# Two halves of weights split ahead of the last turn, and the branch of TensorE with the uncrowded path first

## The reference

```python
p_group = softmax(h @ router_group)            # 4 groups
pg_top, g_idx = top_k(p_group, 1)              # one group for each token
logits_e = (h @ router_expert).reshape(b, s, 4, 4)
sel = logits of the chosen group's 4 experts
top_vals, top_idx = top_k(sel, 2)              # two experts of it
combine = one_hot(expert_id) * pg_top * softmax(top_vals)
for e in range(16):
    hid = silu(h @ w_gate[e]) * (h @ w_up[e])  # 2048 x 512 each
    y = y + combine[:, e] * (hid @ w_down[e])  # 512 x 2048
```

## Time and profile before

| | us |
|---|---|
| median of three runs | 2960.05 (2958.6 to 2963.99) |
| span of the profiled execution | 2960.2 |
| TensorE busy | 2919.3 (99%) |
| TensorE weight loads | 2566.1 (87%) |
| VectorE busy | 1932.5 (65%) |
| ScalarE busy | 1649.3 (56%) |
| stretch from the last attention unit to the first expert unit | 781 to 799.3 |
| experts | 799.3 to 1401 |

### The profile page before, as it was taken

How to read it: one execution, slowest core, us unless ns; L and a number is a source line. 1 busy time by engine, 2 the same in 40 slices (tenths; PEclk the granted TensorE clock), 3 DMA queues, 4 the chain that set the end, 5 groups by cost and what they waited for, 6 DMA issues and landing times.

```text
span 2960.2 us, 40967 instructions
## 1 busy us (share of the span) xinstructions
PE 2919.3 (99%) x16760; PEld 2566.1 (87%) x16760; DVE 1932.5 (65%) x2257; ACT 1649.3 (56%) x1957; POOL 105.6 (4%) x83
## 2 busy tenths in 40 slices
PE   8999999999899999999999999999999999999998
PEld 8988988898777878777999988888899999888886
DVE  6777444535698989898676764555656577555554
ACT  6544444435587877777555544554545654445453
POOL 2222000000000000000000000000000000000000
PEclk9999999999999999999999999999999999999999
DMA  7544566545498989899555556555564555555553
GB/s 267 179 142 161 203 207 237 206 168 174 134 358 311 362 314 357 313 353 317 196 170 187 166 176 197 189 177 184 181 205 143 191 166 185 191 190 190 181 195 128
DMA packets 279930, 632.52 MB, mean 214 GB/s; under 512 B 18953, under 2 KB 32834, under 8 KB 262466
## 3 DMA queue, kind: packets, MB, share of 16 engines
q1 hardware_dynamic: 278274, 624.67, 61.6%
q10 hardware_dynamic: 1184, 4.20, 0.4%
q0 software_dynamic: 288, 1.05, 0.1%
HBM read 622.52 MB, written 7.36 MB: 213 GB/s over the span
## 4 chain that ended last, share of the span: by engine, by line
PE 84%; DVE 6%; issue 5%; ACT 4%; DMA 1%; SPq 0%; POOL 0%; POOLq 0%; ACTq 0%; DVEq 0%
PE pairs L662 17%; PE pairs L664 17%; PE pairs L663 17%; PE pairs L672 8%; PE pairs L676 8%; PE pairs L674 8%; DVE w_lo L1983 3%; PE misc L1143 2%; ACT w_hi L1384 1%; PE misc L821 1%; PE misc L1073 1%; PE misc L1029 1%; ACT scratch L1798 1%; DVE scratch L2664 1%; DMA raw<-in_w_gate_dram 0%
## 5 line engine op out<-in xcount | busy, mean ns | idle before, releaser
L1983 DVE TENSOR_TENSOR w_lo<-raw,w_hi 128x1024 fp32r<-128x1024 f32 x1136 | 1388.1, 1243 | 855.0 <-ACT w_hi L1384 847.0
L1384 ACT ACTIVATE w_hi<-raw 128x1024 fp32r<-128x1024 f32 x1136 | 1183.7, 1059 | 952.6 <-PE pairs L664 585.0
L662 PE MATMUL pairs<-w_hi,a_hi 128*128 128x512 f32 x1664 | 658.5, 396 | 5.4 <-DVE a_lo L2417 2.4
L664 PE MATMUL pairs<-w_hi,a_lo 128*128 128x512 f32 x1664 | 648.4, 390 | 0.0
L663 PE MATMUL pairs<-w_lo,a_hi 128*128 128x512 f32 x1664 | 648.1, 389 | 0.0
L672 PE MATMUL pairs<-a_hi,w_hi 128*128 128x256 f32 x1920 | 551.2, 287 | 6.6 <-DVE w_lo L1983 6.6
L674 PE MATMUL pairs<-a_lo,w_hi 128*128 128x256 f32 x1920 | 544.1, 283 | 0.0
L676 PE MATMUL pairs<-a_hi,w_lo 128*128 128x256 f32 x1920 | 544.0, 283 | 0.0
L662 PEld LDWEIGHTS pairs<-w_hi,a_hi 128*128 128x128 f32 x1664 | 312.5, 188 | 77.7 <-DVE w_lo L1983 11.5
L672 PEld LDWEIGHTS pairs<-a_hi,w_hi 128*128 128x128 f32 x1920 | 369.2, 192 | 11.1 <-DVE w_lo L1983 6.9
L674 PEld LDWEIGHTS pairs<-a_lo,w_hi 128*128 128x128 f32 x1920 | 369.4, 192 | 0.7 <-issue 0.2
(11 more groups left out here) (353 smaller groups left out, 2250.5 us busy)
## 6 DMA issues: line engine op xcount, KB each, us to landing
raw<-in_w_in_dram SPq DMA_DIRECT2D x232, 1024.0 KB, 5.2
raw<-in_w_out_dram SPq DMA_DIRECT2D x80, 1024.0 KB, 5.1
raw<-in_w_gate_dram SPq DMA_DIRECT2D x64, 1024.0 KB, 5.6
raw<-in_w_up_dram SPq DMA_DIRECT2D x64, 1024.0 KB, 5.6
raw<-in_w_down_dram SPq DMA_DIRECT2D x64, 1024.0 KB, 6.1
raw<-in_xattn_wk_dram SPq DMA_DIRECT2D x16, 1024.0 KB, 5.1
raw<-in_xattn_wv_dram SPq DMA_DIRECT2D x16, 1024.0 KB, 5.0
raw<-in_xattn_wq_dram SPq DMA_DIRECT2D x16, 1024.0 KB, 5.1
```

Of the source, the lines that this page charges most:

```text
L662: nc.tensor.matmul(o, hi[:, k, tok], w_hi[:, s, q, :], start=k == 0, stop=False)
L664: m = nc.tensor.matmul(o, lo[:, k, tok], w_hi[:, s, q, :], start=False, stop=last)
L1384: a.activation(w_hi[:, i % HSLOTS], raw[:, i // 2, 2 * (i % 2):2 * (i % 2) + 2, :], ACT.Copy).then_inc(hi_done, 1)
L1983: v.tensor_tensor(w_lo[:, i % HSLOTS], raw[:, i // 2, 2 * (i % 2):2 * (i % 2) + 2, :], w_hi[:, i % HSLOTS].bitcast(F32), ALU.subtract).the ...
```

## The change

ScalarE splits four halves (0 to 3 of the first expert unit) ahead of its wait for the last turn, and none behind `by_row_copy(3)`. VectorE splits three halves ahead of `add_unit("wo", 3)` and the fourth behind it, and none in the two places in the choice. In `slots` the product `slot_of` comes first, then the maximum, then `choose(0)`, and only then the number for the branch. That number is now `roomy`: 1 when the largest count is at most 128. TensorE's branch tests it and has `experts(1)` as its first body and `experts(TT)` as its second.

```diff
-        crowded = SC[:, 12994:12995].bitcast(I32)
+        roomy = SC[:, 12994:12995].bitcast(I32)
...
             pe.wait_ge(crowd_ok, 1)
-            many = nc.values_load(crowded[0:1, 0:1], engines=[pe.engine], min_val=0, max_val=P)
-            with pe.If(many):
+            few = nc.values_load(roomy[0:1, 0:1], engines=[pe.engine], min_val=0, max_val=1)
+            with pe.If(few):
+                experts(1)
+            with pe.Else():
                 experts(TT)
-            with pe.Else():
-                experts(1)
...
-            run(2)
+            run(4)
             act.wait_ge(turned, 16)
...
-            run(2)
             act.wait_ge(rt_x, 1)
             a.activation(rt_ge, rt_gd, ACT.Exp).then_inc(rt_e, 1)
...
             v.tensor_scalar(upto, causal[:], -0.5, None, ALU.is_ge)
-            run(2)
+            run(3)
             add_unit("wo", 3)
+            run(1)
             for k in range(4):
...
                 dve.wait_ge(rank_mm, 1)
-                s1(v.tensor_reduce(fullest, misc[:, 1, 8:12], AX.X, ALU.max))
-                v.tensor_scalar(crowded, fullest, -float(P), 0.0, ALU.add, ALU.max)\
-                 .then_inc(crowd_ok, 1)
                 s1(v.tensor_tensor(slot_of, misc[:, 1, 0:8].rearrange("p (t e) -> p t e", t=TT), rt_og,
                                    ALU.mult))
+                step(v.tensor_reduce(fullest, misc[:, 1, 8:12], AX.X, ALU.max))
                 choose(0)
+                step.wait()
+                v.tensor_scalar(roomy, fullest, float(P), None, ALU.is_le).then_inc(crowd_ok, 1)
...
             group_choice()
             slots()
-            run(1)
             expert_choice()
-            run(1)
             first_lo(0, 0)
```

## The result

The changed kernel takes 2963.89 us (median of 21 runs, 2961.37 to 2973.13), the kernel before 2960.91 us (median of 21, 2958.38 to 2963.99). The ratio is 1.0014, 95% interval 1.0008 to 1.0020: slower by 2.4 to 5.9 us (the two medians lie 3.0 us apart). The forecast was 2960.0 us, no change. The time lies inside the range, but the interval leaves out the forecast: a loss was measured where none was foreseen. The 21 runs of each kernel tell apart less than the 0.2% that the prediction took for the limit.

The account below looks back on a forecast made before the run. TensorE, busy 99%, bounds the kernel; only its wait before the experts, behind the taken branch and VectorE's chain, could be won. 2960.2 − 1.6 + 1.5 = 2960.1, against the median 2960.0 us; range 2957.0 to 2964.5.

Parts of the forecast that it names:

- The branch at the front: TensorE's branch before the experts: not taken, it costs 0.076 us instead of 3.418, hidden by the gathering matmuls.
- VectorE's chain: Before the experts: VectorE's splits of halves 2 and 3 leave the choice; TensorE's first expert matmul comes 1.9 us earlier.
- the first unit: First expert unit: VectorE moves less than TensorE, so `turn_pick` waits 0.3 us and 1.6 us of gain are left.
- The halves split ahead: Around `wo`'s end: ScalarE's and VectorE's early splits fit idle time and cost nothing; without cover, routing starts up to 0.4 us later.
- the transfers: SyncE's transfer for halves 2 and 3 goes at about 783, not 797.6; counted nothing, bounds 2.8 us gain, 1 us loss.
- The jump at the end: End of `experts(1)`, between lru0 0 and lru0 1: a taken jump of 3.42 us, partly hidden by the sequencer's lead.
- The lead is 2.1 us, eighteen matmuls of 0.12 us: Ahead of unit lru0 1: TensorE's sequencer runs 2.1 us ahead of the matmuls, hiding that much of the exit jump.
- 1.5 us lost: Exit jump's net cost: 1.3 us bare beyond the lead plus about 0.2 us for the first issue behind it.
- 0 to 0.1 us: Behind the exit jump, until the next small matmuls: further cost, since little lead is regained but none is needed.
- a second fetch: Named in the chances only: slower by over 0.2%, chance 0.05, needs the clock and the bare jump, or this.
- the rival with a chance of 0.08: At about 1426, TensorE's clock halves for 10.2 us after the bare 1.5 us, losing 4.4 us: 2964.4 us; chance 0.08.
- The upper bound of 3.7 us for a jump with no lead: Exit jump: the most it was said to lose, 3.7 us, if the sequencer's lead counts for nothing.

## Why the prediction was wrong

- **The branch at the front, VectorE's chain, the first unit:** right. 69 ns for 76; the first matmul 2.0 us earlier, counted from the last turn, for 1.9; 0.36 us given back for 0.3; 1.65 us left for 1.6. It held in seven of nine traces of kernels with both parts. In the other two the longer half clock left 0.1 us: a cover had gone that the prediction did not name, the old jump's over the gathering. The mean gain of the nine is 1.14 us against the first trace of before.
- **The halves split ahead, the transfers:** right. ScalarE's split ran from 779.91 for 1.06 us beside an idle engine, SyncE's transfer went out at 782.34 (783 forecast), TensorE's waits for w_lo in the experts were 1.8 us where they had been 2.8, and the stage's length moves by more than that from run to run.
- **The jump at the end:** this step failed. "The lead is 2.1 us, eighteen matmuls of 0.12 us" held (2.13), and so did the length of about 3.4 us (3.4 to 3.9). What failed is the sum behind it, "1.5 us lost", and the line that followed, "0 to 0.1 us" for what comes next. The prediction names "a second fetch" once, among the chances, and gives it no price. The runs show in its place a second charge of this jump: TensorE has the block behind the target only 4.5 to 5.1 us after the jump's end, and the target lay 17 matmuls, 2.3 us, ahead of that block's end. 2.4 us more were bare. With 48 instructions of padding the cost is the predicted 1.5 us. A reading was wrong too, with no effect on the sum: the front jump leads past the first, crowded body, 10,916 instructions and not 5,635, so the jump at the exit is as long as the one read and not longer.
- **The clock:** the rival with a chance of 0.08 was right in kind, wrong in size: 1.5 us, not 4.4, since the clock was down for 3.4 us and not for 10.2. In the two traces in which the clock was down for 6.8 us, the stage lost 2.7 and 2.0 us beyond its idles. There it fell behind one idle of 1.76 or 1.78 us, close to the bare 1.5 us of the rival; behind 1.29, 1.42 and 1.68 us it did not. The 0.200 us for a matmul at the half clock was read from a count that takes in matmuls cut by the window; their starts stand 0.21 apart, and 0.118 at the full clock.
- **The sum:** 1.14 us won and 5.14 lost (mean of 5.93 and 4.35) are 4.0 us; the two ratios of this kernel say 4.1 and 3.6, its medians 3.0 and 4.9. The upper bound of 3.7 us for a jump with no lead was too low because it priced one fetch.
- **What could have been read before:** the old jump at the front shows the late second block as well. It ended at 798.95, the instruction queue moved nothing until 801.7 and then one block in the next 0.2 us:
```profile
q8 instruction: 1, 0.02, 28.1%
```
There it lay under matmuls of 512 columns. I read the branch's row and stopped; the queue's rows behind it, and the target's distance to its block's end, were the missing term.

What stays open: a kernel without the exit's cost should be about 1.1 us faster than before, a ratio of 0.9996. The four comparisons of such kernels gave 1.0005, 0.9999, 1.0000 and 1.0003, each within 0.0009 either way. A gain that small isn't shown in time, only in the traces, and no version here beats the kernel before. Why the lower clock at the front lasts 10.2 us in ten of the 13 traces and 13.6 in three, and after which idle it falls at the exit, was not settled.

## What to carry to other kernels

Moving a far jump does not remove it: ask what lies over its new place, and price both fetches, the target's (3.4 to 3.9 us) and that of the block behind it (4.5 to 5.1 us after the jump's end). Put it where the queued matmuls are wide (18 of 0.227 us covered the first, and 22 the second but for 0.16 us), or where the program ends anyway. And a stall that goes had hidden others: here it had covered the clock's longer dips.

## What was not expected of the hardware

- The cost of a taken far jump depends on where its target lies: 1.5, 4.4 to 5.9 and 6.8 us in the exit stage for three positions 16 to 48 instructions apart.
- The sequencer's lead goes by the number of matmuls and not by time: about 2.13 us at 256 columns in five traces, 18 matmuls of 0.118 us, and at least 3.76 us at 512, so 17 or more of 0.227.
- A far jump past 10,900 instructions or more took 3.38 to 3.90 us in 13 traces, the changed kernel's own 3.80 and 3.54 in two; and the same code of the experts took 584.3 to 590.7 us.
